# The start of an output projection: three hyena halves first, and the norm of y by token sums

## The chip, the core and the metric

The kernel runs on one core of one Trainium2 chip. The metric is the device time of one execution in microseconds (us). Engines: PE is TensorE (PEld its weight loads), DVE is VectorE, ACT is ScalarE, POOL is GpSimd, SP only issues DMAs.

## What is computed

Two layers of a block over 512 latent and 256 context tokens, width 1024. Layer 0 mixes by a bidirectional state-space scan (y) and by a long convolution (g, "hyena"), layer 1 by windowed attention; both end with a gated feed-forward. The change lies in `finish` of layer 0 and in how the first products after a norm are ordered:

```python
def finish(y, z, hy):
    b, L = z.shape[:2]
    y = rmsnorm(y.reshape(b, L, SSD_WIDTH) * jax.nn.silu(z.astype(jnp.float32)), norm_g).astype(z.dtype)
    g = hyena_op(hy, hy_conv_w, hy_conv_b, hy_filt, hy_bias)
    return jnp.concatenate([y, g], axis=-1) @ w_out
# rmsnorm(t, g) = t * rsqrt(mean(t*t, over the width) + 1e-6) * g
# x = x + mod * finish(...); then a norm with gains and shifts, then swiglu
```

## The kernel before

**Products in three parts.** Activations lie transposed: 8 tiles (`KT`) of 128 features by 768 tokens (`TOK`; `SEGS` cuts them into 512 and 256 columns). A float32 product is made of three: weights and activations are each split into a high part (rounded, fp32r) and a low part (the rest), and high x high, high x low and low x high are added in PSUM. `tiles` is that loop: for each tile four matmuls with the high part of the activations, then two with the low part. Eight tiles are called a half here.

**Weight jobs.** `JOBS` lists the weights in the order of use, 16 tiles a job in two halves, loaded by SP into one of 3 slots. VectorE makes the high half (`split_high`, `next_high`, the cast at L1587) in one buffer `WH` of two halves: a half can be cast only when the half of the job before has been multiplied (semaphore `blocks_done`). GpSimd makes the low half (`low`, L2013). TensorE waits for it in `half_ready` and for the PSUM accumulator in `pair_ready` (three accumulators, pairs 0 to 2). An "out0" job is one block of 128 output features: first half of the hyena input, second half of y. For other jobs (`two_blocks`) the halves are two blocks with the same input. `by_tile` gives a pair of waits per tile, for the high part (ScalarE) and the low part (GpSimd) of the input, used where the input is only being made.

**The order around the output projection.** Each engine's program is written out by hand; it runs in order.
- ScalarE copies the 8 high parts of g (L1362), squares the 8 tiles of y (L1368, two buffers), takes the root over 128x768 (L1370), then copies the high parts of the normed y (L1373).
- VectorE, after the scan, casts both halves for block 0, makes the 8 gate products y * silu(z) (L1813), waits for the root, takes the reciprocal (L1815) and multiplies each tile of y by gain and norm (L1817). Then `res` adds each block to the residual (L1844) and its squares to a running sum (L1510, L1511).
- GpSimd makes both low halves of weights for block 0, the 8 low parts of g and the 8 of y (L2155), then low halves one by one.
- TensorE multiplies block 0's hyena half, sums the squares over features with a matrix of ones (`norm_sums`, L551, 32 matmuls, the result on all partitions), multiplies block 0's half of y, then blocks 1 to 7.

**Other norms** use `norm_sum`: the squares summed in `T[:, 3]` are reduced per token by 6 small matmuls (L560) to 12 columns, root and reciprocal work on these, and 6 matmuls with the identity (L565) spread the result into PSUM (`NP`). VectorE then multiplies tile by tile (L1576) and applies gain and shift (L1578); ScalarE and GpSimd make the high (L1184) and low parts (L2026), and the first job behind it takes them with `by_tile`, its second block after its first.

Of the kernel before, what the change touches and what calls it, by code (L numbers as in the profile page):

```python
# [6 lines left out]
D = 1024  # L7
# [71 lines left out]
def plan():  # L79

    used, turn, out, last = [0, 0, 1], 0, [], None
    for kind, layer, _ in JOBS:
# [72 lines left out]
def build_kernel(nc, A, out):  # L155
# [6 lines left out]
    with ctx:  # L162
# [155 lines left out]
        def dvec(name, base, i, step=1):  # L318
# [16 lines left out]
            sq_ready sq_mm norm_sqrt norm_mul hn_ready conv_first  # L335
# [10 lines left out]
         sq_ready, sq_mm, n_sqrt, n_mul, hn_ready, cv_act,  # L346
# [115 lines left out]
        def _(pe):  # L462
# [31 lines left out]

            def two_blocks(gs, i, rhs, segs=SEGS, between=None, by_tile=None):
                for b in range(2):
                    half_ready(gs, i, b)
                    u = pair_ready(gs, i, b)
                    tiles(gs, pair(u), b, KT, rhs, segs, True, True, by_tile if b == 0 else None)
                    if b == 0 and between:  # L500
                        between()
# [44 lines left out]
            def norm_sums(segs=SEGS):  # L546

                for k in range(KT):
                    pe.wait_ge(sq_ready, k + 1)
                    for a, b in segs:  # L550
                        ins = mm(NP[:, a:b], C[:, ONES, :], T[:, k % 2, a:b], start=k == 0, stop=k == KT - 1)  # L551
                    ins.then_inc(sq_mm, 1)

            def norm_sum(n, segs=SEGS):
# [3 lines left out]
                pe.wait_ge(sums_ready, n + 1)  # L558
                for t in range(tiles):
                    ins = mm(NS[:, 2 * t:2 * t + 2], T[:, 3, t * P:t * P + P], C[:, ONES, 0:2],  # L560
                             start=True, stop=True)
                ins.then_inc(n_summed, 1)
                pe.wait_ge(n_rec, n + 1)
# [3 lines left out]
                ins.then_inc(n_spread, 1)  # L567
# [330 lines left out]
            def turn(s0, chunks, last):  # L898

                for d in range(2):  # L900
# [38 lines left out]
            half_ready([G0], 0, 0)  # L939
            first = pair(pair_ready([G0], 0, 0))  # L940
            tiles([G0], first, 0, KT, mixed, SEGS, True, False, mixed_waits)

            norm_sums()
            half_ready([G0], 0, 1)
            tiles([G0], first, 1, KT, lambda k: mixed(KT + k), SEGS, False, True,
                  [lambda k, wait=wait: wait(KT + k) for wait in mixed_waits])

            def res_block(name, rhs, segs=SEGS, by_tile=None, skip=0):
                def body(gs, i, r):
                    if isinstance(r, int) and r < skip:  # L950
                        return
# [3 lines left out]
            res_block("out0", mixed, by_tile=mixed_waits, skip=1)  # L955
# [140 lines left out]
        def _(act):  # L1096
# [266 lines left out]

            for k in range(KT):
                act.wait_ge(yz_ready, k + 1)
                if k >= 2:
                    act.wait_ge(sq_mm, k - 1)
# [106 lines left out]
        def _(dve):  # L1474
# [337 lines left out]
            for k in range(KT):  # L1812
                TT(XBC[:, k, :], XBC[:, k, :], Z[:, k, :], ALU.mult).then_inc(yz_ready, 1)  # L1813
            dve.wait_ge(n_sqrt, 2)
            ch.link(dve.reciprocal(T[:, 3, :], T[:, 2, :]))  # L1815
            for k in range(KT):
                STT(XBC[:, k, :], XBC[:, k, :], vec("sng", k), T[:, 3, :], ALU.mult, ALU.mult).then_inc(n_mul, 1)  # L1817
# [5 lines left out]
            def res(name, layer, m, segs, squares=True):  # L1823
# [5 lines left out]

                def body(gs, i, r):  # L1830
                    if not two:
                        next_high(gs, i, 0)
                    for b in range(2 if two else 1):
                        if two or b == 0:
                            next_high(gs, i, b if two else 1)
                        k = r if not two else 2 * r + b
# [6 lines left out]
                        for j, (a, e) in enumerate(segs):  # L1843
                            ins = STT(x[:, a:e], pair(u)[:, a:e], column(layer, m, k, j), x[:, a:e],  # L1844
                                      ALU.mult, ALU.add)
                        ins.then_inc(pair_free[u], 1)
# [6 lines left out]
                else:  # L1853
                    peel = 2 if name == "out0" else 0
                    job_turns(dve, name, 8, body, ch, 2 * SLOTS if squares else 0, peel)
# [114 lines left out]
        def _(pool):  # L1970
# [179 lines left out]

            for n in range(2 * KT):
# [4 lines left out]
            next_low("out0", 8, 2)  # L2156
# [98 lines left out]
def _layout(a):  # L2255
# [7 lines left out]
    for g, (kind, layer, n) in enumerate(JOBS):  # L2263
# [13 lines left out]
        elif kind == "out0":  # L2277
            wall[g] = np.roll(tiles(a["hy_out_w"][0], n * P), KT, 1)
            continue
        elif kind == "up":  # L2280
# [68 lines left out]
```

## Time and profile before

| | before |
|---|---|
| median of 3 runs | 2413.69 us |
| lowest, highest | 2411.80, 2418.44 us |
| profiled execution | 2418.78 us |
| its span (first to last instruction) | 2417.0 us |
| busy: PE, PEld, DVE, ACT, POOL | 92, 72, 40, 17, 35% |
| granted TensorE clock, mean of the span | 0.933 of 2.4 GHz |

Times in the rows count from the start of the span. A timeline row gives start, duration, engine, line, operation, output and inputs, count, and in brackets how long the engine idled before and what released it; a row with a count above 1 merges neighbours, and its duration is that of all. The end of a matmul is modelled, so neighbours overlap a little.

### The profile page before, as it was taken

How to read it: one execution, taken by the hardware profiler on the slowest of the kernel's cores; microseconds unless marked ns; L12 is line 12 of the kernel's file. 1: busy time of each engine (PE TensorE's matmuls, PEld its weight loads, DVE VectorE, ACT ScalarE, POOL GpSimd, SP SyncE). 2: the span in 40 equal slices, each digit the busy share in tenths (PEclk: the TensorE clock that was granted, in tenths of full speed). 3: DMA queues.
4: the chain of work that ended last, by engine and by line, in shares of the span. 5: the costliest groups of instructions: out<-in, count | busy, mean ns of one | idle time of the engine just before them, and what ended most of it. 6: DMA issues, size and time to landing. Idle time of an engine off the chain costs nothing. (4 is left out here: it accounts for less than half of the span.)

```text
span 2417.0 us, 30280 instructions
## 1 busy us (share of the span) xinstructions
PE 2217.1 (92%) x11978; PEld 1734.4 (72%) x11978; DVE 960.0 (40%) x1284; ACT 413.7 (17%) x769; POOL 856.9 (35%) x460
## 2 busy tenths in 40 slices
PE   7959998899998996997999999998787998999997
PEld 2436865688887774885888888887475666888886
DVE  3555354321234767335122112133525655322334
ACT  1211111001244553001000000000103631100110
POOL 0264353512223756323222332222421124444442
PEclk8777998999998997997999999999788998999998
DMA  8312432333311001110111221112110002223222
GB/s 302 135 52 96 152 111 101 107 113 126 102 44 53 1 2 43 56 67 26 61 61 48 74 71 61 53 60 70 61 45 18 1 28 69 95 78 112 91 82 73
DMA packets 50750, 181.52 MB, mean 75 GB/s; under 512 B 5815, under 2 KB 6071, under 8 KB 49688
## 3 DMA queue, kind: packets, MB, share of 16 engines
q1 hardware_dynamic: 48288, 163.60, 20.2%
q10 hardware_dynamic: 1848, 13.52, 1.5%
q0 software_dynamic: 512, 2.95, 0.3%
q8 instruction: 75, 1.23, 0.2%
q14 instruction: 27, 0.22, 0.0%
HBM read 177.95 MB, written 2.10 MB: 74 GB/s over the span
## 5 line engine op out<-in xcount | busy, mean ns | idle before, releaser
L2013 POOL TENSOR_TENSOR weights_lo<-weights,weights_hi 128x1024 fp32r<-128x1024 f32 (+1 forms) x232 | 514.4, 2218 | 1042.8 <-DVE weights_hi L1587 1042.8
L492 PE MATMUL psum<-normed_lo,weights_hi 128*128 128x512 f32 x1856 | 550.9, 360 | 12.0 <-POOL normed_lo L2026 11.9
L1587 DVE CAST weights_hi<-weights 128x1024 fp32r<-128x1024 f32 (+1 forms) x232 | 163.9, 707 | 921.1 <-PE psum L492 786.4
L487 PE MATMUL psum<-normed_hi,weights_hi 128*128 128x512 f32 (+1 forms) x1152 | 425.2, 369 | 16.1 <-ACT normed_hi L1184 16.1
L488 PE MATMUL psum<-normed_hi,weights_lo 128*128 128x512 f32 (+1 forms) x1152 | 404.8, 365 | 0.0
L492 PEld LDWEIGHTS psum<-normed_lo,weights_hi 128*128 128x128 f32 x1856 | 306.0, 193 | 43.7 <-POOL normed_lo L2026 26.3
L487 PEld LDWEIGHTS psum<-normed_hi,weights_hi 128*128 128x128 f32 x1152 | 221.6, 192 | 74.4 <-ACT normed_hi L1184 15.2
L487 PE MATMUL psum<-normed_first_hi,weights_hi 128*128 128x512 f32 x704 | 248.5, 353 | 16.1 <-POOL weights_lo L2013 9.3
L488 PEld LDWEIGHTS psum<-normed_hi,weights_lo 128*128 128x128 f32 x1152 | 222.7, 193 | 38.3 <-issue 1.5
L488 PE MATMUL psum<-normed_first_hi,weights_lo 128*128 128x512 f32 x704 | 226.7, 343 | 0.0
L487 PE MATMUL psum<-hidden_hi,weights_hi 128*128 128x512 f32 (+1 forms) x528 | 189.1, 358 | 0.0
L488 PE MATMUL psum<-hidden_hi,weights_lo 128*128 128x512 f32 (+1 forms) x528 | 178.9, 354 | 0.0
L487 PEld LDWEIGHTS psum<-normed_first_hi,weights_hi 128*128 128x128 f32 x704 | 135.8, 193 | 57.3 <-issue 10.8
L492 PE MATMUL psum<-hidden_lo,weights_hi 128*128 128x512 f32 (+1 forms) x528 | 160.4, 358 | 0.0
L488 PEld LDWEIGHTS psum<-normed_first_hi,weights_lo 128*128 128x128 f32 x704 | 136.3, 194 | 17.6 <-issue 1.2
L487 PEld LDWEIGHTS psum<-hidden_hi,weights_hi 128*128 128x128 f32 x528 | 99.1, 188 | 23.5
L488 PEld LDWEIGHTS psum<-hidden_hi,weights_lo 128*128 128x128 f32 x528 | 99.3, 188 | 15.0
L487 PE MATMUL psum<-mixed_hi,weights_hi 128*128 128x512 f32 (+1 forms) x256 | 90.5, 354 | 14.2 <-ACT mixed_hi L1373 8.0
L1618 DVE SCALAR_TENSOR_TENSOR temps<-psum,vectors,temps 128x511 f32<-128x511 f32 x112 | 63.8, 612 | 98.6 <-ACT temps L1198 97.6
L492 PEld LDWEIGHTS psum<-hidden_lo,weights_hi 128*128 128x128 f32 x528 | 87.1, 188 | 8.9
L1389 ACT ACTIVATE temps<-psum 128x768 f32<-128x768 f32 (+1 forms) x44 | 31.1, 707 | 355.7 <-PE psum L492 355.7
L1393 ACT ACTIVATE hidden_hi<-temps 128x768 f32 (+3 forms) x44 | 32.5, 740 | 342.9 <-DVE temps L1872 342.9
(281 smaller groups left out, 3015.1 us busy)
## 6 DMA issues: line engine op xcount, KB each, us to landing
weights<-in_wall SPq DMA_DIRECT2D x264, 512.0 KB, 4.0
weights<-in_wall SPq DMA_DIRECT2D x32, 384.0 KB, 3.2
weights<-in_wall SPq DMA_DIRECT2D x32, 320.0 KB, 3.0
residual<-in_xT ACTq DMA_DIRECT2D x2, 3072.0 KB, 10.4
phase<-in_tab ACTq DMA_DIRECT2D x3, 1280.0 KB, 7.0
out_T<-normed SPq DMA_DIRECT2D x2, 1024.0 KB, 4.3
normed<-in_window ACTq DMA_DIRECT2D x1, 1536.0 KB, 16.7
normed<-in_window POOLq DMA_DIRECT2D x1, 1536.0 KB, 7.7
```

What stands on the lines that cost most here:

```text
L487: mm(acc[:, lo:hi], WH[:, b, k, :], high[:, lo:hi], start=st, stop=False)
L488: mm(acc[:, lo:hi], WL[:, s, HALF * b + k, :], high[:, lo:hi], start=False, stop=False)
L492: ins = mm(acc[:, lo:hi], WH[:, b, k, :], low[:, lo:hi], start=False, stop=en)
L1389: run(T[:, 0, lo:hi], pair(0)[:, lo:hi], ACT.Silu).then_inc(pair_free[0], 1)
L1393: run(at_row(HIDH, r)[:, lo:hi], T[:, 1, lo:hi], ACT.Copy).then_inc(hid_hi, 1)
L1587: dve.tensor_copy(WH[:, b, 0:n, :], W[:, s, HALF * b:HALF * b + n, :]).then_inc(w_hi, 1)
L1618: ins = STT(t[:, a:e], p[:, a + shift:e + shift], w, t[:, a:e], ALU.mult, ALU.add)
L2013: TT(WL[:, s, at, :], W[:, s, at, :], WH[:, b, 0:width(gs[0], b), :].bitcast(f32), ALU.subtract).then_inc(w_lo, 1)
```

## The change

1. **Jobs.** The first three out0 jobs become "halves" jobs: (hyena of block 0, hyena of block 1), (hyena of block 2, y of block 0), (y of block 1, y of block 2). Blocks 3 to 7 follow as before, as stage out0b.
2. **Both blocks by tile.** `both_by_tile` takes two accumulators and does the first six tiles for both halves, then tiles 6 and 7 for the one and for the other. It serves the first halves job and, through `two_blocks(..., by_tile=...)`, the first job of the first stage, of the q projection and of each feed-forward's up projection.
3. **Norm of y by token sums.** ScalarE squares y into PSUM (`NP` and `TP` in turn), VectorE adds the squares into `T[:, 3]`, TensorE reduces them behind tile 5 and spreads the reciprocal root behind tile 7 of the first half. `norm_sums` and the work on 128x768 go. VectorE multiplies with the norm in PSUM.
4. **Order.** GpSimd waits for all gate products before its first low part of g. The low halves for the second job stand behind y's low parts 2 and 4 on GpSimd, and their casts behind y's tiles 2 and 4 on VectorE.

The number of products is the same. The diff, cut to its core:

```diff
-    stage("out0", [("out0", 0, n) for n in range(8)])
+    stage("out0", [("halves", 0, ((0, 1), (1, 1))), ("halves", 0, ((2, 1), (0, 0))), ("halves", 0, ((1, 0), (2, 0)))])
+    stage("out0b", [("out0", 0, n) for n in range(3, 8)])
...
+            def both_by_tile(gs, i, rhs, segs, by_tile, after=None, last=True, together=6):
+                s = gs[0] % SLOTS
+                accs = []
+                for b in range(2):
+                    half_ready(gs, i, b)
+                    accs.append(pair(pair_ready(gs, i, b)))
+                order = [(k, (0, 1)) for k in range(together)] + [(k, (b,)) for b in range(2) for k in range(together, KT)]
+                for k, blocks in order:
+                    if blocks[0] == 0:
+                        by_tile[0](k)
+                    high, low = rhs(k)
+                    for b in blocks:
+                        for lo, hi in segs:
+                            mm(accs[b][:, lo:hi], WH[:, b, k, :], high[:, lo:hi], start=k == 0, stop=False)
+                            mm(accs[b][:, lo:hi], WL[:, s, HALF * b + k, :], high[:, lo:hi], start=False, stop=False)
+                    if blocks[0] == 0:
+                        by_tile[1](k)
+                    for b in blocks:
+                        for lo, hi in segs:
+                            ins = mm(accs[b][:, lo:hi], WH[:, b, k, :], low[:, lo:hi], start=False,
+                                     stop=last and k == KT - 1)
...
-            norm_sums()
...
+            def between_tiles(k, blocks):
+                if k == 5 and blocks == (0, 1):
+                    pe.wait_ge(yz_sums, 1)
+                    token_sums(6).then_inc(yz_summed, 1)
+                if k == 7 and blocks == (0,):
+                    pe.wait_ge(yz_rec, 1)
+                    token_spread(6).then_inc(yz_spread, 1)
+            both_by_tile([G0], 0, mixed, SEGS, mixed_waits, between_tiles, False)
+            half_ready([G0 + 1], 0, 0)
+            pe.wait_ge(yz_added, KT)
+            tiles([G0 + 1], pair(pair_ready([G0 + 1], 0, 0)), 0, KT, mixed, SEGS, True, False)
+            for g, b, u in ((G0 + 1, 1, 0), (G0 + 2, 0, 1), (G0 + 2, 1, 2)):
+                half_ready([g], 0, b)
+                tiles([g], pair(u), b, KT, gated, SEGS, False, True, gated_waits if u == 0 else None)
...
-                run(T[:, k % 2, :], XBC[:, k, :], ACT.Square).then_inc(sq_ready, 1)
-            act.wait_ge(sq_mm, KT)
-            run(T[:, 2, :], NP, ACT.Sqrt, scale=1.0 / D, bias=vec("eps", 0)).then_inc(n_sqrt, 1)
+                run(TP if k % 2 else NP, XBC[:, k, :], ACT.Square).then_inc(yz_square, 1)
+            act.wait_ge(yz_summed, 1)
+            root()
```

On GpSimd, from the end of the scan, the program was this (`weights_lo`: low halves; `hyena_lo`, `ssd_lo`: low parts of g and of y):

```order
L2013 TENSOR_TENSOR weights_lo<-weights,weights_hi 128x1024 [waits weights_hi_ready] x2
L2155 TENSOR_TENSOR hyena_lo<-phase,mixed_hi 128x768 [waits mixed_hi] x8
L2155 TENSOR_TENSOR ssd_lo<-phase,mixed_hi 128x768 [waits mixed_hi] x8
L2013 TENSOR_TENSOR weights_lo<-weights,weights_hi 128x1024 [waits weights_hi_ready] x4
```

and is now, at the same place of the same engine:

```order
L2086 TENSOR_TENSOR weights_lo<-weights,weights_hi 128x1024 [waits weights_hi_ready] x2
L2229 TENSOR_TENSOR hyena_lo<-phase,mixed_hi 128x768 [waits mixed_hi,yz_ready]
L2229 TENSOR_TENSOR hyena_lo<-phase,mixed_hi 128x768 [waits mixed_hi] x7
L2229 TENSOR_TENSOR ssd_lo<-phase,mixed_hi 128x768 [waits mixed_hi] x3
L2086 TENSOR_TENSOR weights_lo<-weights,weights_hi 128x1024 [waits weights_hi_ready]
L2229 TENSOR_TENSOR ssd_lo<-phase,mixed_hi 128x768 [waits mixed_hi] x2
L2086 TENSOR_TENSOR weights_lo<-weights,weights_hi 128x1024 [waits weights_hi_ready]
L2229 TENSOR_TENSOR ssd_lo<-phase,mixed_hi 128x768 [waits mixed_hi] x3
```

The first low part of g has a wait for the gate products (`yz_ready`), and two low halves of weights have moved in between the low parts of y.

On VectorE, from the casts behind the scan (`phase` holds y, `temps` and `psum` the norm), the program was:

```order
L1587 CAST weights_hi<-weights 128x1024 [waits w_loaded11]
L1813 TENSOR_TENSOR phase<-phase 128x768 x8
L1815 RECIPROCAL temps<-temps 128x768 [waits norm_sqrt]
L1817 SCALAR_TENSOR_TENSOR phase<-phase,vectors,temps 128x768 [waits dve_order]
L1817 SCALAR_TENSOR_TENSOR phase<-phase,vectors,temps 128x768 x7
```

and is now:

```order
L1632 CAST weights_hi<-weights 128x1024 [waits w_loaded11]
L1858 TENSOR_TENSOR phase<-phase 128x768 x8
L1866 COPY temps<-psum 128x768 [waits yz_square]
L1864 TENSOR_TENSOR temps<-temps,psum 128x768 [waits yz_added,yz_square] x7
L1869 MEMSET mark 128x1 [waits yz_added]
L1871 RECIPROCAL temps<-temps 128x12 [waits norm_sqrt]
L1874 SCALAR_TENSOR_TENSOR phase<-phase,vectors,psum 128x768 [waits yz_spread]
L1874 SCALAR_TENSOR_TENSOR phase<-phase,vectors,psum 128x768 x2
L1632 CAST weights_hi<-weights 128x1024 [waits w_loaded20,blocks_done]
L1874 SCALAR_TENSOR_TENSOR phase<-phase,vectors,psum 128x768 x2
L1632 CAST weights_hi<-weights 128x1024 [waits w_loaded21,blocks_done]
L1874 SCALAR_TENSOR_TENSOR phase<-phase,vectors,psum 128x768 x3
```

Eight operations on the squares have come in, the reciprocal has shrunk to 12 columns, the norm is read from PSUM, and two casts stand between the multiplications.

## Rows read from the trace of the kernel before

**Rows 1.** Page, part 1: busy us, share of the span, instructions.
```profile
PE 2217.1 (92%) x11978; PEld 1734.4 (72%) x11978; DVE 960.0 (40%) x1284; ACT 413.7 (17%) x769; POOL 856.9 (35%) x460
```
**Rows 2.** Waits, 905 to 975: us in total, times, longest.
```profile
PE psum L492 <- POOL hyena_lo L2155: 9.0, 7, 3.9
```
**Rows 3.** Timeline of TensorE, 905 to 975: start us, us.
```profile
909.47 0.79 PE L487 MATMUL psum<-mixed_hi,weights_hi 128*128 128x512 f32 x1 [4.39 <-POOL weights_lo L2013]
...
932.64 10.86 PE L551 MATMUL psum<-temps,consts 128*128 128x512 f32 x32
951.50 0.77 PE L487 MATMUL psum<-mixed_hi,weights_hi 128*128 128x512 f32 x1 [8.00 <-ACT mixed_hi L1373]
...
972.98 0.47 PE L487 MATMUL psum<-mixed_hi,weights_hi 128*128 128x512 f32 x1 [1.78 <-POOL weights_lo L2013]
```
**Rows 4.** Busy time by stretch, then the cast behind the projection's last matmul.
```profile
core 0: us, PE busy (x) PEld busy (x) DVE busy (x) ACT busy (x) POOL busy (x), PEclk, DMA share, GB/s
...
1000.00:1092.00 92.00, 92.00 (x527) 80.41 (x527) 28.84 (x31) 0.00 (x0) 26.50 (x11) 1.00 0.19 63
...
1092.42 0.69 DVE L1587 CAST weights_hi<-weights 128x1024 fp32r<-128x1024 f32 x1 [7.62 <-PE psum L492]
```
**Rows 5.** VectorE: timeline, then L1817 by line (ns min/median/max, starts).
```profile
907.13 21.08 DVE L1813 TENSOR_TENSOR phase<-phase 128x768 f32<-128x768 f32 x8
944.47 4.95 DVE L1815 RECIPROCAL temps<-temps 128x768 f32<-128x768 f32 x1 [16.26 <-ACT temps L1370]
...
L1817 DVE SCALAR_TENSOR_TENSOR phase<-phase,vectors,temps x8: 1012/2572/2584, 949.5 to 962.3; 128x768 f32<-128x768 f32 x8
```
**Rows 6.** Timeline of VectorE and GpSimd, 970 to 997.
```profile
971.24 2.15 DVE L1587 CAST weights_hi<-weights 128x1024 fp32r<-128x1024 f32 x1 [4.18 <-PE psum L492]
...
992.23 1.14 DVE L1844 SCALAR_TENSOR_TENSOR residual<-psum,mods,residual 128x512 f32<-128x512 f32 x2
...
995.65 0.96 DVE L1511 TENSOR_TENSOR temps<-temps 128x768 f32<-128x768 f32 x1
...
992.39 2.40 POOL L2013 TENSOR_TENSOR weights_lo<-weights,weights_hi 128x1024 fp32r<-128x1024 f32 x1 [5.94 <-DVE weights_hi L1587]
```
**Rows 7.** GpSimd: timeline, then L2155 by line.
```profile
906.69 5.75 POOL L2013 TENSOR_TENSOR weights_lo<-weights,weights_hi 128x1024 fp32r<-128x1024 f32 x2 [3.11 <-DVE weights_hi L1587]
912.40 19.25 POOL L2155 TENSOR_TENSOR hyena_lo<-phase,mixed_hi 128x768 fp32r<-128x768 f32 x8
...
L2155 POOL TENSOR_TENSOR hyena_lo<-phase,mixed_hi x8: 1817/2528/2538, 912.4 to 929.8; 128x768 fp32r<-128x768 f32 x8
```
**Rows 8.** Timeline: a square of y; sums and spread of a later norm.
```profile
935.86 0.84 ACT L1368 ACTIVATE temps<-phase 128x768 f32<-128x768 f32 x1 [0.45 <-PE psum L551]
...
1097.69 2.72 PE L560 MATMUL psum<-consts,temps 128*128 128x2 f32 x12 [5.31 <-DVE mark L1858]
1101.04 2.93 PE L565 MATMUL psum<-consts,temps 128*128 128x128 f32 x12 [0.62 <-DVE temps L1568]
```
**Rows 9.** Busy time by stretch, after the idle 8 us.
```profile
950.00:960.00 10.00, 7.13 (x19) 5.40 (x20) 10.00 (x7) 4.35 (x6) 8.57 (x4) 0.50 0.00 0
```
**Rows 10.** Timelines: next job's first low half and first matmul, four norms.
```profile
212.92 2.40 POOL L2013 TENSOR_TENSOR weights_lo<-weights,weights_hi 128x1024 fp32r<-128x1024 f32 x1 [6.27 <-DVE weights_hi L1587]
...
218.87 0.50 PE L487 MATMUL psum<-normed_first_hi,weights_hi 128*128 128x512 f32 x1
...
1134.17 2.40 POOL L2013 TENSOR_TENSOR weights_lo<-weights,weights_hi 128x1024 fp32r<-128x1024 f32 x1 [1.88 <-DVE weights_hi L1587]
...
1142.32 0.39 PE L487 MATMUL psum<-normed_hi,weights_hi 128*128 128x512 f32 x1
...
1724.39 2.39 POOL L2013 TENSOR_TENSOR weights_lo<-weights,weights_hi 128x1024 fp32r<-128x1024 f32 x1 [3.62 <-DVE weights_hi L1587]
...
1728.19 0.40 PE L487 MATMUL psum<-normed_hi,weights_hi 128*128 128x512 f32 x1
...
2038.58 2.38 POOL L2013 TENSOR_TENSOR weights_lo<-weights,weights_hi 128x1024 fp32r<-128x1024 f32 x1 [1.36 <-DVE weights_hi L1587]
...
2043.18 0.39 PE L487 MATMUL psum<-normed_hi,weights_hi 128*128 128x512 f32 x1
```

More of the change, by code:

```diff
@@ L81, in plan @@
     used, turn, out, last = [0, 0, 1], 0, [], None
-    for kind, layer, _ in JOBS:
+    for kind, layer, what in JOBS:
+        if kind == "halves":
+            out.append([(block, used[block]) for block, hyena in what if hyena])
+            for block, hyena in what:
+                used[block] += hyena
+            last = kind
+            continue
         n = job_blocks(kind)
@@ L498, in two_blocks @@
                     u = pair_ready(gs, i, b)
-                    tiles(gs, pair(u), b, KT, rhs, segs, True, True, by_tile if b == 0 else None)
+                    tiles(gs, pair(u), b, KT, rhs, segs, True, True)
                     if b == 0 and between:
@@ L558, in norm_sum, with token_sums @@
                 pe.wait_ge(sums_ready, n + 1)
+                token_sums(tiles).then_inc(n_summed, 1)
+                pe.wait_ge(n_rec, n + 1)
+                token_spread(tiles).then_inc(n_spread, 1)
+            def token_sums(tiles):
                 for t in range(tiles):
@@ L561, in norm_sum, with token_spread @@
                              start=True, stop=True)
-                ins.then_inc(n_summed, 1)
-                pe.wait_ge(n_rec, n + 1)
+                return ins
+            def token_spread(tiles):
                 for t in range(tiles):
@@ L1813, in _ @@
                 TT(XBC[:, k, :], XBC[:, k, :], Z[:, k, :], ALU.mult).then_inc(yz_ready, 1)
+            for k in range(KT):
+                dve.wait_ge(yz_square, k + 1)
+                square = TP if k % 2 else NP
+                if k:
+                    dve.wait_ge(yz_added, k)
+                    ins = TT(T[:, 3, :], T[:, 3, :], square, ALU.add)
+                else:
+                    ins = dve.tensor_copy(T[:, 3, :], square)
+                ins.then_inc(yz_added, 1)
+            dve.wait_ge(yz_added, KT)
+            dve.memset(MARK[:, 0:1], 0.0).then_inc(yz_sums, 1)
             dve.wait_ge(n_sqrt, 2)
-            ch.link(dve.reciprocal(T[:, 3, :], T[:, 2, :]))
+            dve.reciprocal(RS[1][:, 0:12], RS[0][:, 0:12]).then_inc(yz_rec, 1)
+            dve.wait_ge(yz_spread, 1)
             for k in range(KT):
-                STT(XBC[:, k, :], XBC[:, k, :], vec("sng", k), T[:, 3, :], ALU.mult, ALU.mult).then_inc(n_mul, 1)
+                STT(XBC[:, k, :], XBC[:, k, :], vec("sng", k), NP, ALU.mult, ALU.mult).then_inc(n_mul, 1)
+                if k in (2, 4):
+                    next_high([G0], 0, k // 2 - 1)
             def column(layer, m, k, j):
@@ L1828, in res, with residual @@
                     ch.link(dve.memset(T[:, 3, lo:hi], 0.0))
+                def residual(x, u, k):
+                    for j, (a, e) in enumerate(segs):
+                        ins = STT(x[:, a:e], pair(u)[:, a:e], column(layer, m, k, j), x[:, a:e],
+                                  ALU.mult, ALU.add)
+                    ins.then_inc(pair_free[u], 1)
+                if name == "out0":
+                    next_high([G0 + 1], 0, 0)
+                    next_high([G0 + 1], 0, 1)
+                    for k in range(3):
+                        residual(X[:, k, :], k, k)
+                        read([G0 if k < 2 else G0 + 1], 0, k if k < 2 else 0, dve)
+                        ch.link(add_squares(X[:, k, :], lo, hi))
+                        if k < 2:
+                            next_high([G0 + 2], 0, k)
                 def body(gs, i, r):
@@ L1835, in body @@
                             next_high(gs, i, b if two else 1)
-                        k = r if not two else 2 * r + b
+                        k = r + 3 if name == "out0" else r if not two else 2 * r + b
                         if two:
@@ L1842, in body @@
                             dve.wait_ge(blocks_done, 2 * len(JOBS))
[L1843 to L1846, printed above, removed]
+                        residual(x, u, k)
                         if squares:
@@ L2155, in _ @@
                 TT(YGL[j][:, k, :], src, YGH[:, j, k, :].bitcast(f32), ALU.subtract).then_inc(mix_lo, 1)
-            next_low("out0", 8, 2)
+                if n in (KT + 2, KT + 4):
+                    low([G0 + 1], 0, (n // 2 - 5,))
+            for g in (G0 + 1, G0 + 2):
+                low([g + 1], 0)
+            next_low("out0b", 5)
             def out_low(item):
@@ L2279, in _layout @@
             continue
+        elif kind == "halves":
+            two = [(a["hy_out_w"][0][D * hyena:D * hyena + D], block * P) for block, hyena in n]
         elif kind == "up":
```

41 lines of the change are left out of this document (19 added, 22 removed).

## The prediction, made before the changed kernel was run

> **What bounds the kernel now.** I read the busy shares first: TensorE is busy for 92% of the span [rows 1], so what can be won is the time in which it waits, or runs at its lower clock. Then the waits of TensorE in the stretch where the output projection of layer 0 begins: the largest is for the low parts of the hyena output, 9.0 us in 7 waits [rows 2]. Then the timeline of that stretch, engine by engine.
>
> TensorE starts block 0 at 909.5, needs until 932.6 for its first half, sums the squares of y for 10.9 us, idles 8.0 us, starts the second half at 951.5 and block 1 at 973.0 [rows 3]. A half is 8 tiles of 6 matmuls. With TensorE busy throughout at a granted clock of 1.00 (2.4 GHz) it takes 8.4 us: the stretch 1000 to 1092 is 92.00 of 92.00 us busy with 527 matmuls, 48 to a half [rows 4]; it ends with the projection. So two halves, 16.8 us of work, have taken 63.5 us.
>
> Why: VectorE's eight gate products take 21.1 us [rows 5], 2.6 each, while GpSimd works; the same form alone, two inputs in SBUF, takes 0.96 [rows 6]. GpSimd's low parts take 2.5 us beside them and 1.82 alone [rows 7]. Then the norm: a reciprocal of 128x768, 4.95 us, and eight multiplications, 2.57 us as a rule and 1.01 the shortest, again against GpSimd [rows 5, 7]. But an operation of VectorE with one input in PSUM is not slowed: the residual STT at 992.23 takes 1.14 us for both segments inside a low part of 2.40 us [rows 6].
>
> **The change, part by part.** All times are on the clock of the profiled execution.
>
> Start. TensorE now needs both low halves of the weights before its first matmul; the second is done at 912.4 [rows 7], so it starts 3.0 us later than at 909.5.
>
> Gate products. GpSimd still splits the weights until 912.4, beside the first two products, which end at 912.8 as before. It then waits for all eight. Six products at 0.96 end at 918.6. Queued behind GpSimd's wait are all its low parts, and TensorE waits for the first: it comes at 918.6 + 1.82 = 920.4, where it came at 914.9 (TensorE's wait on it is in [rows 2]). The eight low parts end at 918.6 + 8 x 1.82 = 933.2, against 931.6. So this edit alone costs TensorE's first tile 5.5 us; its price is paid by the norm, which comes earlier.
>
> Norm. ScalarE squares into PSUM in 0.84 [rows 8], VectorE adds eight times with one input in PSUM. That form (TT, one input in PSUM) is nearest to the residual STT, not slowed; I take 0.96 to 1.0 each, so the sums are ready at 918.6 + 8 x 0.97 = 926.4. The upper bound is 2.6 each, 939.4, as for two inputs in SBUF [rows 5]. The 32 matmuls of 10.9 us fall away. For them come two groups of six small ones (each in two passes, so 12 records): the same groups at a later norm take 2.7 and 2.9 us [rows 8], with matmuls that go at 1.2 GHz there; at 2.4 I take half, 2.9 together. The square root and the reciprocal are now 12 columns; they lie beside tiles 6 and 7 (2.1 us), and the 4.95 us reciprocal goes.
>
> TensorE's 16 tile halves. A tile half is 1.05 us at 2.4 GHz [rows 4], at 1.2 twice that. The high part of tile 0 for both blocks is done before 920.4 (1.3 tile halves), so 14.7 are left. After an idle time the clock is low: 950 to 960, after the 8.0 us, was granted 0.50 though TensorE was busy for 7.13 us of it [rows 9]. I take 6 us at 1.2 GHz (2.9 tile halves) and 11.8 x 1.05 = 12.4 us at 2.4, with 2.9 for the small matmuls: the end is 920.4 + 6 + 12.4 + 2.9 = 941.7. GpSimd at 1.82 per tile is ahead of TensorE at 2.1. The spread, on which VectorE's multiplications wait, is done two tile halves before the end, at 939.6. Call it S.
>
> The new wait. TensorE's next half (block 2, hyena) needs a low half of weights, which GpSimd makes behind three low parts of y. VectorE: three STTs with the norm in PSUM at 1.0 (the fastest of the eight was that long) to S + 3.0, then the cast. A cast that met GpSimd took 2.15 against 0.69 alone [rows 4, 6], so S + 4.5 to 5.2; not critical. ScalarE's first copy ends at S + 2.0. GpSimd: three low parts to S + 7.5, of which one loses 0.6 to 0.7 to the cast, then 2.4 for the weights, again with up to 0.7 for the second cast: S + 10.5 to 11.2. I take 10.9. TensorE resumes at 950.5 after 8.8 us idle. Here the Trainium skill speaks against the two casts: SBUF — State Buffer, Who interferes with whom, says that VectorE and GpSimd share one pair of ports as an exclusive lock, and that the one which comes second is fully blocked. By that rule neither cast could slip in beside a low part and the forecast would be 2383; the trace's two casts agree with it (2.15 against 0.69 us).
>
> After it 14 halves, 117.6 us. Nothing of them waits: every cast is released by the end of a half, and cast and low part (3.1 us) lie beside the next half of 8.4. The second half of that job (y for block 0) needs y's last low part at about S + 23, and starts at S + 10.9 + 8.4 = S + 19 with its first tiles. The restart at 1.2 GHz costs 2.5 us (5 us at half speed). End: 950.5 + 117.6 + 2.5 = 1070.6. Before, the 14 halves went from 973.0 to 1092.4, 119.4 us; the cast that waits for the last matmul is the last of [rows 4]. **Gain 21.8 us.** DMAs: SP's queue has the same loads in the same order; the weights of the second and third of the new jobs are loaded at the end of the scan as now, and the next load waits for the first of the 16 tile halves' blocks, some 20 us before its cast. GpSimd's queue is moved past no DMA.
>
> The four starts after a norm. Now the first job of the first stage, of the two feed-forwards and of the q projection does both blocks on each of the first six tiles. The tiles still come as VectorE and GpSimd give them (both unchanged), so block 0 ends when it did, and block 1 ends two tile halves later instead of eight. But the next job needs its low half of weights, which hangs on block 0's end alone and stays where it is. The gain is thus the next job's start less the end of that low half [rows 10]:
> - first stage: 218.87 - 215.32 = 3.5, less some 1.5 for a clock that falls in the 4 us of waiting: 2.0. This low half hangs on a load that is issued at block 0's end.
> - feed-forward 0: 1142.32 - 1136.57 = 5.7; the wait is short, the clock stays.
> - q projection: 1728.19 - 1726.78 = 1.4, less 1.4 for the clock: 0. VectorE is held up there by a wait for the rope table before its cast, not by TensorE.
> - feed-forward 1: 2043.18 - 2040.96 = 2.2.
>
> Sum 9.9 us; its ends are 3 (clock falls at each) and 13 (nowhere).
>
> Total 21.8 + 9.9 = 31.7 us. The span of 2417.0 becomes 2385.3, the execution of 2418.8 becomes 2387.1. That execution is 5.1 above the median of the runs (2413.7), so the forecast for the median is 2382.0.
>
> **The rivals.**
> *VectorE and GpSimd still collide* with PSUM inputs, or the wait for the gate products does not do what it says. For it: every SBUF pair is slowed. Against: the STT at 992.23 [rows 6]. Then the adds last to 939.4, TensorE waits for the sums before tile 6, S comes near 945.5 and the restart at S + 13, 958.5: 8 us less, 2390. The gate wait useless (products slow anyway, 2.6 each) would give the same order, 9.6 us.
> *The starts give nothing*, since the low half of the next weights comes later or the clock falls in each: 2392. Against: block 0's last tile is paced as before.
> *The clock stays up* through the wait for weights and in every start: 5 us more, 2376. The row of 950 to 960 speaks against it.
> *Slower*: the restart after 8.8 us of idle doesn't bring the clock back. Place: the 14 halves behind 950.5. A half at 1.2 GHz costs 8.4 us more; from the fourth such half on (31.7 / 8.4 = 3.8) the kernel is slower than before, and with all 14 it is 2497. Against: after the 8.0 us idle in the trace, and with a TensorE that was still waiting for tiles, the clock was 1.00 again from 1000 on [rows 4, 9].
>
> **How the numbers follow.** Main case 0.66 (2374 to 2390). Collision 0.13 (2390), starts give nothing 0.10 (2392), clock stays up 0.07 (2376), slower 0.02, small effect through something unseen 0.02. The predicted time is the main case's 2382. The range 2372 to 2396 takes in all but the last two and the tails of the first ones. A measurement here can tell about 0.3%, 7 us: faster than 2406.5 in 0.95, within 0.3% in 0.03, slower in 0.02.
>
> **What would show it.** Gate products of about 2.6 us for two and 0.96 for six; adds and STTs of about 1 us beside low parts of 1.82; the sums in TensorE behind tile 5 without a wait; an idle time of 8 to 9 us before block 2, released by the low weights; last matmul of the projection some 22 us earlier; second jobs behind the norms released by the low weights. It would be wrong if the adds take over 2 us, or if TensorE's clock in the 16 tile halves stays at 1.2 GHz (12 us more), or if the starts show the same times for the second jobs.

## The result, and the profile after

The changed kernel takes **2384.24 us** (median of 4 runs, 2383.03 to 2385.71) against 2414.68 for the kernel before, run beside it (2411.80 to 2418.44). The ratio is 0.9865, its 95% interval 0.9849 to 0.9880: 30.4 us less, against a forecast of 2382.0 in a range of 2372 to 2396. A second set of four runs, e12 below, gave 2383.82.

The profiled execution took 2385.36 us, its span 2383.5 against 2417.0 before. The first two lines are part 1 of its page (as [rows 1]) and the row of TensorE's granted clock in 40 slices; then come TensorE's four longest waits between 895 and 1064 us (engine, line, releaser: us in total, times, longest), as [rows 2]:

```profile
PE 2180.6 (91%) x11970; PEld 1720.1 (72%) x11970; DVE 950.4 (40%) x1293; ACT 413.2 (17%) x770; POOL 848.9 (36%) x460
...
PEclk7879999899998997998999999998898998999998
...
PE psum L495 <- POOL weights_lo L2086: 8.5, 1, 8.5
PE psum L518 <- POOL weights_lo L2086: 7.6, 1, 7.6
PE psum L524 <- POOL hyena_lo L2229: 4.9, 1, 4.9
PE psum L924 <- DVE normed L1805: 1.2, 1, 1.2
```

TensorE is busy for 36.5 us less; its idle time has hardly moved (199.9 us before, 202.9 after). The seven waits for low parts of g are one, and the long wait is now for the weights of block 2, as forecast.

TensorE's timeline of the stretch (start us, us), the counterpart of [rows 3]. L518, L519 and L524 are tiles of the first job, L596 the token sums, L602 the spread, L495 the first tile of block 2, L1632 (VectorE) the cast that opens the stage:

```profile
906.84 0.76 PE L518 MATMUL psum<-mixed_hi,weights_hi 128*128 128x512 f32 x1 [7.56 <-POOL weights_lo L2086]
...
914.60 1.65 PE L524 MATMUL psum<-hyena_lo,weights_hi 128*128 128x512 f32 x4 [4.86 <-POOL hyena_lo L2229]
...
928.64 1.39 PE L596 MATMUL psum<-consts,temps 128*128 128x2 f32 x12
...
932.08 1.50 PE L602 MATMUL psum<-consts,temps 128*128 128x128 f32 x12
...
944.22 0.79 PE L495 MATMUL psum<-mixed_hi,weights_hi 128*128 128x512 f32 x1 [8.52 <-POOL weights_lo L2086]
```

VectorE and GpSimd beside it, the counterparts of [rows 5, 7]:

```profile
900.11 1.29 DVE L1632 CAST weights_hi<-weights 128x1024 fp32r<-128x1024 f32 x2
901.32 11.33 DVE L1858 TENSOR_TENSOR phase<-phase 128x768 f32<-128x768 f32 x8
912.57 0.95 DVE L1866 COPY temps<-psum 128x768 f32<-128x768 f32 x1
913.63 7.31 DVE L1864 TENSOR_TENSOR temps<-temps,psum 128x768 f32<-128x768 f32 x7
921.00 0.06 DVE L1869 MEMSET mark<- 128x1 f32 x1
930.37 0.23 DVE L1871 RECIPROCAL temps<-temps 128x12 f32<-128x12 f32 x1 [9.31 <-ACT temps L1222]
933.62 2.87 DVE L1874 SCALAR_TENSOR_TENSOR phase<-phase,vectors,psum 128x768 f32<-128x768 f32 x3 [3.02 <-PE psum L602]
936.40 1.56 DVE L1632 CAST weights_hi<-weights 128x1024 fp32r<-128x1024 f32 x1
...
939.73 2.22 DVE L1632 CAST weights_hi<-weights 128x1024 fp32r<-128x1024 f32 x1
...
912.73 14.40 POOL L2229 TENSOR_TENSOR hyena_lo<-phase,mixed_hi 128x768 fp32r<-128x768 f32 x8 [6.11 <-DVE phase L1858]
935.59 5.80 POOL L2229 TENSOR_TENSOR ssd_lo<-phase,mixed_hi 128x768 fp32r<-128x768 f32 x3 [8.46 <-ACT mixed_hi L1418]
941.37 2.80 POOL L2086 TENSOR_TENSOR weights_lo<-weights,weights_hi 128x1024 fp32r<-128x1024 f32 x1
```

The stage opens at 900.11 where it opened at 905.92, so 5.8 us must be taken off the prediction's times when they are laid beside these. The eight gate products take 11.33 us (21.08 before), the adds 7.31 / 7 = 1.04 us each beside low parts of 14.40 / 8 = 1.80. The sums are ready at 921.00, but TensorE comes to them at 928.64 only: 7.6 us to spare.

**Where the time went.** I cut the span at events that both kernels have: the token sums of the norms and the cast that opens the output projection. Three of these rows are

```profile
170.49 2.69 PE L596 MATMUL psum<-consts,temps 128*128 128x2 f32 x12 [10.90 <-POOL vectors L2078]
...
1068.86 2.72 PE L596 MATMUL psum<-consts,temps 128*128 128x2 f32 x12 [5.14 <-DVE mark L1931]
...
1986.19 1.87 PE L596 MATMUL psum<-consts,temps 128*128 128x2 f32 x8 [4.66 <-DVE mark L1931]
```

and the table has the differences. The last columns are the experiments' profiled executions ("6 tiles together": e2 to e5, e7 and e12; "4 together": e6 and e8 to e10); in them a stage whose code is the same shows how far one execution differs from another.

| stretch, us | before | after | e1: starts undone | e11: starts alone | others, first job of 6 tiles together | others, 4 together |
|---|---|---|---|---|---|---|
| up to the first token sums | 172.0 | 170.5 | 171.8 | 169.3 | 167.4 to 171.5 | 168.5 to 171.3 |
| first norm to the cast | 733.9 | 729.6 | 733.7 | 732.8 | 728.6 to 732.9 | 727.8 to 732.1 |
| cast to feed-forward 0 | 191.8 | 168.8 | 168.8 | 191.7 | 169.2, 169.9, unless edited | 168.9, unless edited |
| feed-forward 0 to q projection | 587.5 | 581.2 | 587.5 | 581.7 | 581.0 to 582.1 | 582.8 to 583.9 |
| q projection to feed-forward 1 | 334.1 | 336.1 | 333.5 | 336.6 | 332.0 to 337.8 | 330.5 to 333.7 |
| feed-forward 1 to the last sums | 383.8 | 383.5 | 383.9 | 383.5 | 382.4 to 384.3 | 381.9 |

Before less after: 1.6 + 4.3 + 23.0 + 6.3 - 2.0 + 0.4, with nothing behind the last sums, is the 33.5 us between the two spans, but for rounding. The 1.6 lie ahead of any changed instruction.

### The profile page after: what moved, and what is told of

Read it like the earlier page. It is cut to its first block and busy times, and to the rows that moved or that the text cites. A ratio compares the mean times of both kernels' runs of the same rounds, so it can differ in the third digit from the quotient of the medians.

```text
span 2383.5 us, 30200 instructions
## 1 busy us (share of the span) xinstructions
PE 2180.6 (91%) x11970; PEld 1720.1 (72%) x11970; DVE 950.4 (40%) x1293; ACT 413.2 (17%) x770; POOL 848.9 (36%) x460
## 5 line engine op out<-in xcount | busy, mean ns | idle before, releaser
L1632 DVE CAST weights_hi<-weights 128x1024 fp32r<-128x1024 f32 (+1 forms) x232 | 167.4, 723 | 900.8 <-PE psum L500 748.3
L500 PE MATMUL psum<-normed_lo,weights_hi 128*128 128x512 f32 x1760 | 508.5, 352 | 0.0
L495 PE MATMUL psum<-normed_hi,weights_hi 128*128 128x512 f32 x1088 | 395.4, 363 | 5.7 <-POOL weights_lo L2086 5.7
L496 PE MATMUL psum<-normed_hi,weights_lo 128*128 128x512 f32 x1088 | 373.9, 358 | 0.0
L500 PEld LDWEIGHTS psum<-normed_lo,weights_hi 128*128 128x128 f32 x1760 | 284.9, 190 | 16.8
L495 PEld LDWEIGHTS psum<-normed_hi,weights_hi 128*128 128x128 f32 x1088 | 206.4, 190 | 56.7 <-POOL weights_lo L2086 4.8
L495 PE MATMUL psum<-normed_first_hi,weights_hi 128*128 128x512 f32 (+1 forms) x672 | 234.0, 348 | 10.4 <-POOL weights_lo L2086 9.9
L496 PEld LDWEIGHTS psum<-normed_hi,weights_lo 128*128 128x128 f32 x1088 | 206.9, 190 | 35.5 <-issue 1.8
L496 PE MATMUL psum<-normed_first_hi,weights_lo 128*128 128x512 f32 (+1 forms) x672 | 214.6, 341 | 0.0
L495 PE MATMUL psum<-hidden_hi,weights_hi 128*128 128x512 f32 (+1 forms) x528 | 189.0, 358 | 0.0
L495 PEld LDWEIGHTS psum<-normed_first_hi,weights_hi 128*128 128x128 f32 x672 | 128.3, 191 | 46.2 <-POOL weights_lo L2086 12.0
L496 PEld LDWEIGHTS psum<-normed_first_hi,weights_lo 128*128 128x128 f32 x672 | 128.6, 191 | 16.4 <-issue 1.0
L495 PEld LDWEIGHTS psum<-hidden_hi,weights_hi 128*128 128x128 f32 x528 | 99.1, 188 | 23.4
L495 PE MATMUL psum<-mixed_hi,weights_hi 128*128 128x512 f32 x224 | 76.4, 341 | 8.5 <-POOL weights_lo L2086 8.5
```

The source lines that it names most:

```text
L495: mm(acc[:, lo:hi], WH[:, b, k, :], high[:, lo:hi], start=st, stop=False)
L496: mm(acc[:, lo:hi], WL[:, s, HALF * b + k, :], high[:, lo:hi], start=False, stop=False)
L500: ins = mm(acc[:, lo:hi], WH[:, b, k, :], low[:, lo:hi], start=False, stop=en)
L1632: dve.tensor_copy(WH[:, b, 0:n, :], W[:, s, HALF * b:HALF * b + n, :]).then_inc(w_hi, 1)
```

## The experiments

Each set of runs had its own runs of the kernel before, with medians of 2417.0 to 2417.2. The median of one kernel moves by up to 3 us between sets (before: 2414.7 in the first, 2417.2 in a later one), so below I give the stage's length in the profiled execution too, which is steadier: 168.8 to 169.9 us in the five executions whose output projection is that of the changed kernel.

**e1, the four starts undone.** `two_blocks` again does block 0 whole, then block 1:

```diff
-                if by_tile:
-                    both_by_tile(gs, i, rhs, segs, by_tile)
-                    return
+                    tiles(gs, pair(u), b, KT, rhs, segs, True, True, by_tile if b == 0 else None)
```

> The changed kernel, except that the four first jobs after a norm (first stage, both feed-forwards, q projection) do block 0 whole and then block 1, as before; the start of the output projection stays changed. My theory (the starts are worth what lies between the next job's low half and its first matmul): their share was 10 to 12 us (3.5 first stage, 5.6 and 2 to 3 the feed-forwards, about 0 the q projection), so this kernel takes 2394 to 2397 us against 2384 of the changed one. Rival (the starts give little and the output projection gave all 30 us): 2384 to 2387. In the trace the next jobs' first matmuls follow the low halves by 3.5, 5.7, 1.4 and 2.2 us again.

2394.11 us (2393.28 to 2394.86), ratio to before 0.9904 (0.9889 to 0.9919). That is 9.9 us over the changed kernel, where the prediction had 9.9 for the starts; the projection's stage is the same to 0.1 us. It rules out the rival, by which the output projection gave all 30 us.

**e11, the starts alone**, in the kernel before.

> The kernel before, with only the four first jobs after a norm done for both blocks on each of the first six tiles; the output projection is as before. If the two parts of the change are independent, this kernel is faster than the one before by what undoing them cost, 9.9 us: 2404 to 2408 us against 2414 to 2417. Rival (the starts win more when the projection is not changed, or nothing at all without it): outside 2402 to 2410.

2407.46 against 2417.15, ratio 0.9966 (0.9954 to 0.9978): 9.7 us, with an interval of 5 to 11. As far as that interval can tell, the two parts add up and do not lean on each other.

**e2, GpSimd does not wait for the gate products** (its `pool.wait_ge(yz_ready, KT)` is taken out).

> The changed kernel without GpSimd's wait for all eight gate products: it goes from the weights straight to the low parts. My theory (two inputs in SBUF collide with GpSimd, and the norm hangs on the products): the products take 21 us again instead of 11.3, the sums are ready some 9 us later, the first low part comes some 5.5 us earlier but this wins nothing, since TensorE waits before its seventh tile; about 2391 to 2393 us. Rival (products and low parts only swap places, TensorE gets its first tile 5.5 us earlier and keeps it): 2379 to 2384.

2392.29 us (2391.40 to 2395.85), ratio 0.9901 (0.9886 to 0.9917), 8 us more than with the wait. Its VectorE timeline, and TensorE's at the sums:

```profile
901.50 21.20 DVE L1858 TENSOR_TENSOR phase<-phase 128x768 f32<-128x768 f32 x8
...
931.16 2.72 PE L596 MATMUL psum<-consts,temps 128*128 128x2 f32 x12 [8.25 <-DVE mark L1869]
```

TensorE hardly waits for low parts of g (0.3 us in two waits, 4.9 in one with the gate wait) and gives it all back in a wait of 8.25 us at the sums. The stage is 174.8 us for 168.8, 6 of the 8 us. So the gate wait is a real part of the gain.

**e3, the squares in SBUF:**

```diff
-                run(TP if k % 2 else NP, XBC[:, k, :], ACT.Square)
+                run(T[:, k % 2, :], XBC[:, k, :], ACT.Square)
...
-                square = TP if k % 2 else NP
+                square = T[:, k % 2, :]
```

> The changed kernel with the squares of y written by ScalarE to two buffers in SBUF instead of PSUM, so that VectorE's adds have both inputs in SBUF. Nothing else differs. Collision theory: the adds go from 0.9 to 1.0 us to some 2.5 each and GpSimd's low parts of the hyena output beside them from 1.80 to some 2.5; the sums are ready some 11 us later (932 for 921 on the trace's clock), TensorE idles before its seventh tile, and the kernel takes 2393 to 2397 us. Rival (the place of the input does not matter, the adds were fast for another reason): 2384 to 2386, adds at 1.0 us.

2387.67 us (2386.39 to 2392.25), ratio 0.9877 (0.9862 to 0.9892): the mechanism is there, but the cost is 3.4 us by medians, where I had expected 9 to 13. The profiled execution is the slowest of the four, 2392.25 us.

```profile
913.21 17.45 DVE L1864 TENSOR_TENSOR temps<-temps 128x768 f32<-128x768 f32 x7
...
912.72 19.61 POOL L2229 TENSOR_TENSOR hyena_lo<-phase,mixed_hi 128x768 fp32r<-128x768 f32 x8 [6.11 <-DVE phase L1858]
...
930.84 2.72 PE L596 MATMUL psum<-consts,temps 128*128 128x2 f32 x12 [1.89 <-DVE mark L1869]
```

The adds take 2.49 us each instead of 1.0, the low parts beside them 2.45 instead of 1.80. Only the place of the squares differs, so this settles the collision. The Trainium skill (SBUF — State Buffer, Who interferes with whom) says that a VectorE instruction with two SBUF inputs contends with a GpSimd instruction that reads SBUF and that one with at most one SBUF input, outside the two-port modes, does not; both halves agree with this pair of runs. The sums are ready 9.7 us later (930.7 for 921.0), but 7.6 of them were to spare: TensorE starts them 2.2 us later. The rest of the stage's 6.5 us (175.2 for 168.8) is mostly its clock, low again for the sums (2.72 for 1.39 us) and the tiles behind them: the granted clock from 930 to 935 is 0.59, and 1.00 in the changed kernel. Why this execution lost 3 us more than the medians show is open. My expectation had charged the whole delay to TensorE.

**e4, the norm read from a copy in SBUF.** ScalarE copies `NP` to `T[:, 2, :]`, and VectorE's eight STTs read that.

> The changed kernel, but ScalarE first copies the spread norm from PSUM to SBUF, and VectorE's eight multiplications read the copy: both their tensors are then in SBUF. Collision theory: the three multiplications before GpSimd's first low part of y stay near 1 us, those beside low parts go to 2 to 2.6 us, and low parts of y beside them to some 2.5; with 1.0 us for the copy the restart of TensorE at block 2 comes 2 to 4 us later, which is 2386 to 2389 us. Rival (no collision): only the copy shows, 2385, multiplications at 1.0 us.

2388.66 us (2384.69 to 2390.85), ratio 0.9891 (0.9873 to 0.9909); the stage 172.0 us, 3.3 more.

```profile
932.25 2.88 DVE L1876 SCALAR_TENSOR_TENSOR phase<-phase,vectors,temps 128x768 f32<-128x768 f32 x3 [3.87 <-ACT temps L1417]
...
942.82 8.12 DVE L1876 SCALAR_TENSOR_TENSOR phase<-phase,vectors,temps 128x768 f32<-128x768 f32 x3
...
934.22 8.13 POOL L2231 TENSOR_TENSOR ssd_lo<-phase,mixed_hi 128x768 fp32r<-128x768 f32 x3 [9.30 <-ACT mixed_hi L1420]
...
945.15 0.80 PE L495 MATMUL psum<-mixed_hi,weights_hi 128*128 128x512 f32 x1 [11.68 <-POOL weights_lo L2088]
```

The three STTs that start before GpSimd does take 0.96 us each and the last three, beside it, 2.7 (0.95 with the norm in PSUM). GpSimd's three low parts take 8.13 instead of 5.80 us, and TensorE waits 11.68 instead of 8.52. Here nothing was to spare: of the 3.2 us, the copy is 0.8 (VectorE starts 34.4 us behind the stage's opening, 33.5 without it) and GpSimd's slower low parts are 2.3. By medians the cost is 4.4 us.

**e5, the weights of block 2 first:**

```diff
+            next_high([G0], 0, 0)
             dve.wait_ge(yz_spread, 1)
...
-                if k in (2, 4):
-                    next_high([G0], 0, k // 2 - 1)
+                if k == 2:
+                    next_high([G0], 0, 1)
...
-                if n in (KT + 2, KT + 4):
-                    low([G0 + 1], 0, (n // 2 - 5,))
+                if n in (KT - 1, KT + 1):
+                    low([G0 + 1], 0, (0 if n < KT else 1,))
```

> The changed kernel with the weights of block 2 split first: VectorE's cast comes before its first multiplication with the norm (not behind the third) and GpSimd's low half of them before the low parts of y (not behind the third); the second half of that job is cast behind the third multiplication and split behind the second low part of y. My theory (the 8.5 us in which TensorE idles before block 2 are GpSimd's chain of three low parts and the weights, counted from the spread of the norm): the idle time shrinks to 0 to 2 us, the clock does not fall, and TensorE loses up to 1 us to the low parts of y in the next half; 2373 to 2377 us. Rival (the time is only moved: y's last low parts come later and TensorE waits for them in the half of y of block 0): 2382 to 2385.

2377.37 us (2374.76 to 2380.18), ratio 0.9837 (0.9824 to 0.9851): 7 us faster than the changed kernel by medians (the two intervals just touch), and its stage is 161.8 us, 7.0 less.

```profile
933.15 0.69 DVE L1632 CAST weights_hi<-weights 128x1024 fp32r<-128x1024 f32 x1 [1.68 <-PE psum L524]
...
933.92 2.39 POOL L2087 TENSOR_TENSOR weights_lo<-weights,weights_hi 128x1024 fp32r<-128x1024 f32 x1 [5.92 <-DVE weights_hi L1632]
...
952.49 0.62 PE L500 MATMUL psum<-ssd_lo,weights_hi 128*128 128x512 f32 x2 [0.45 <-POOL ssd_lo L2230]
...
954.27 0.61 PE L500 MATMUL psum<-ssd_lo,weights_hi 128*128 128x512 f32 x2 [0.47 <-POOL ssd_lo L2230]
...
956.59 0.50 PE L495 MATMUL psum<-mixed_hi,weights_hi 128*128 128x512 f32 x1 [1.70 <-POOL weights_lo L2087]
...
930.00:940.00 10.00, 10.00 (x65) 8.94 (x65) 6.43 (x8) 2.99 (x5) 5.93 (x3) 1.00 0.32 104
```

The cast needs only block 0's end, not the norm. The 8.5 us idle are gone, TensorE is busy through 930 to 940 at a granted clock of 1.00, and 2.6 us come back in three waits of the next half, all of them for GpSimd, which is now the bound there.

**e6, four tiles together at the starts instead of six.**

> The changed kernel, but at the four starts behind a norm only the first four tiles, not six, are done for both blocks; block 1 then has four tile halves left behind block 0's end instead of two. My theory (the next job hangs on block 0's end, cast and low half, not on block 1): the next jobs start when they did, TensorE's waits before them (1.6, 0, 3.8 and 1.9 us) shrink to 0, 0, 1.7 and 0, and at most a clock that falls less gives 1 to 2 us: 2382 to 2385. Rival (what is left of block 1 is on the path): 2.1 us more at each start, 2388 to 2392.

2383.06 us (2379.88 to 2389.64), ratio 0.9867 (0.9844 to 0.9890): no difference in total, but some that cancel. Feed-forward 1 gains 1.8 us on average (381.9, in all four kernels with this edit): its wait of 1.88 became 0.56 and the clock stayed at 1.00. The q projection's stretch is 330.8 us, against 332.9 to 337.8 with six. Feed-forward 0 loses 1.7 (583.2 for 581.5 on average): there TensorE does block 1's four last tile halves from 1107.9 to 1113.9, the first two of them at 1.2 GHz, 1.92 us each, while the low half of the next weights is done at 1111.3. So they outlast it by 2.6 us. That is the rival's mechanism, at one of the four starts.

**e7, the rope table early**: its load ahead of the low parts, VectorE's wait for it behind the first q job's casts.

> The changed kernel with the rope table loaded before the low parts of the q projection's norm instead of behind them, and VectorE's wait for it behind the casts of the first q job instead of ahead of them. My theory (the q start gave nothing, since the wait for the table held the cast for some 2.5 us): the cast follows the end of block 0 directly, the next q job's low half ends 2 to 2.5 us earlier, TensorE waits 1 to 1.5 us in place of 3.8, and the kernel takes 2380 to 2382 us. Rival (the casts wait for something else): 2384.

2380.60 us (2378.82 to 2390.24), ratio 0.9862 (0.9841 to 0.9884). By medians that is 3 to 4 us less than the changed kernel; by the ratio the two can't be told apart. TensorE's wait before the second q job:

```profile
1690.53 0.79 PE L495 MATMUL psum<-normed_hi,weights_hi 128*128 128x512 f32 x1 [0.68 <-POOL weights_lo L2087]
```

It is 0.68 for 3.84 us, so the table did hold the cast.

**e8, e5 to e7 together.**

> The changed kernel with three edits together: weights of block 2 cast and split ahead of y, only four tiles for both blocks at the starts, and the rope table early with VectorE's wait for it behind the casts. If their effects add up, the time is that of the changed kernel less 7 us for the first, less 0 to 2 for the second and 2 to 4 for the third: 2371 to 2375 us. Rival (what one wins is lost again at the other places): 2376 to 2378.

**2372.43 us** (2369.71 to 2374.86), ratio 0.9823 (0.9808 to 0.9837), 12 us below the changed kernel and within the 2371 to 2375 of effects that add up. Neither e9 nor e10 can be told from it.

**e9 and e10** edit e8 further: GpSimd waits for six gate products instead of eight; VectorE makes the last two low parts of y.

> The kernel with the three edits together, in which GpSimd waits for six gate products, not eight. The squares' sums were ready some 6 us before TensorE came to them. My theory (that spare time can be spent): the first low part comes 1.9 us earlier, two gate products beside low parts take 2.5 us instead of 0.96, the sums are ready 3 us later, still before TensorE's seventh tile, and the stage is shorter by 1.5 to 1.9 us: 2370 to 2371.5 us. Rival (TensorE at its lower clock is what paces the tiles, so an earlier first tile is given back in waits): 2372 to 2373.5.

> The kernel with the three edits together, in which VectorE, not GpSimd, makes the last two of y's eight low parts, behind its cast for block 1. After the cast is moved ahead, TensorE waits 0.45, 0.47 and 1.70 us for GpSimd's low parts and weights in the next half. My theory (GpSimd is the bound there, busy from 934 to 957 without a gap): its queue gets 3.6 us shorter, VectorE's two take 1 to 2.5 us each in its idle time, the three waits shrink to under 1 us together: 1.5 to 2.5 us less, 2370 to 2371. Rival (VectorE's operations hold up GpSimd's by as much as they take off it): 2372 to 2373.5.

e9 2372.78 us (0.9816, 0.9798 to 0.9833), e10 2372.31 us (0.9817, 0.9797 to 0.9837). Both medians lie in the range that I had given to the rivals. In its own trace each shortens the stage, from 161.0 to 159.6 and 159.8 us, which is less than I wanted and about as much as one and the same stage moves from one execution to another: neither theory nor rival is shown. In e10 VectorE's two low parts take 5.10 us, 2.55 each beside GpSimd; TensorE's waits in that half shrink from 2.6 to 0.8 us, as expected, but the stage gets only 1.2 shorter.

**e12, the changed kernel again.**

> The changed kernel once more, unchanged, beside the others, to see how far its median moves from one set of runs to the next. If such a median is good to 1.5 us: 2382.5 to 2386. Rival (sets of runs differ by more, and differences of 3 us between kernels of different sets mean nothing): outside that.

2383.82 us (2381.99 to 2384.84), within what was expected of a second set. The kernel before moved by more: 2414.68 in the first set, 2417.15 in this one.

## Why the prediction held, point by point

**The total.** The gain is 30.4 us by the first set and 33.3 by the last (2417.15 less 2383.82), for a forecast of 31.7. The forecast of the time itself took off 5.1 us, by which the profiled execution of the kernel before lay above the median of three runs. Above the later medians of 9 and 17 runs, 2417.0 to 2417.2, it lies by only 1.7, and with these the same gain would have given 2385.4. So which of the two comes nearer to the measured 2384.2 says nothing of the mechanism; the parts do.

**The projection: 23.0 us for a forecast of 21.8.** Laid beside the prediction's times less 5.8, nearly every step is where it was put: first low part used at 914.60 (914.6), sums ready at 921.00 (920.6), spread read from 933.62 (S = 933.8), restart 944.22 (944.7) after 8.52 us idle (8.8). The two casts slipped in at 1.56 and 2.22 us, and GpSimd lost 0.4 us to each, so the restart lies 10.6 us behind the spread for 10.9 forecast. Steps that stood on one row of another operation held: the adds were not slowed, as the residual STT was not, and e3 shows that it is the place of the squares; the STTs took 1.0, and e4 shows the same of the norm. That the chain of three low parts and the weights is behind the 8.5 us is shown by e5, which took it away.

**The gate wait** paid for itself as argued (e2), through the sums and not through the low parts.

**The collision rival** was priced at 8 us on the assumption that both adds and STTs collide. e3 and e4 together cost 6.5 + 3.3 us of stage and 3.4 + 4.4 by medians, so its size was about right. Alone, the adds cost less than their delay, since 7.6 us were to spare. The rival in the prediction already had this: its sums are 13 us later, but its spread only 5.9 (945.5 for 939.6; e3 has 5.5). It is my expectation for e3 that forgot it and charged TensorE with the whole delay.

**The starts: the sum is right, two of its terms are not.** e1 and e11 give 9.9 and 9.7 us for a forecast of 9.9. By stage, on average, they were 3.2 in the first (733.8 in the two executions with the old order, 730.6 the mean of twelve with a new one; forecast 2.0), 6.0 in feed-forward 0 (587.5 for 581.5; forecast 5.7), -1.6 in the q projection (333.8 in two, 335.4 the mean of seven), within its scatter (0), and 0.1 in feed-forward 1 (2.2). These add up to 7.7, which the interval of e11 (5 to 11) takes in; that the medians met 9.9 to a tenth is luck. The failed step is who pays for the clock. Lines of the changed kernel at the first stage and at feed-forward 1 (in the stretches, the second number behind the times is TensorE busy, and third from the end is the granted clock):

```profile
213.83 0.50 PE L495 MATMUL psum<-normed_first_hi,weights_hi 128*128 128x512 f32 x1 [1.62 <-POOL weights_lo L2086]
...
214.00:219.00 5.00, 5.00 (x29) 4.39 (x30) 2.04 (x1) 0.00 (x0) 3.98 (x2) 1.00 0.91 287
...
2008.06 0.49 PE L495 MATMUL psum<-normed_hi,weights_hi 128*128 128x512 f32 x1 [1.88 <-POOL weights_lo L2086]
...
2007.00:2012.00 5.00, 3.94 (x12) 3.13 (x13) 3.79 (x3) 0.63 (x1) 3.31 (x2) 0.74 0.48 165
2012.00:2017.00 5.00, 5.00 (x22) 4.01 (x21) 0.69 (x1) 0.60 (x1) 0.62 (x1) 0.92 0.05 9
```

- I charged the first stage 1.5 us, for a clock that falls in 4 us of waiting. In nine of the twelve executions TensorE waits 2.0 us or less there and the clock stays at 1.00; in the other three (e2, e5, e11) it waits 3.1 to 3.4 us, and the 5 us behind the wait are at 0.68. The cast that lies 179.0 us behind the token sums with the old order lies at 175.5 to 176.0 in the nine and at 176.9 to 177.2 in the three. So the forecast's 3.5 and 2.0 are both there, and it had picked the rarer one.
- I charged feed-forward 1 nothing. It starts its next job 2.0 us earlier and loses that again: in seven of the eight executions with six tiles together the clock falls behind the wait of 1.9 us. In the eighth (e3) it stays at 1.00 behind the same wait, and that stretch is the shortest of the eight, 382.4 us for 383.5 to 384.3 (383.8 and 383.9 with the old order). e6 shows it from the other side.

The two errors have opposite signs: the first stage gave 1.2 us more than forecast, feed-forward 1 gave 2.1 less. The old order has only two such executions, so the split between the first stage and the q projection is good to some 2 us, no better.

**The slower rival** did not come: after 8.52 us idle the first 3.8 us were at 1.2 GHz (forecast: 5), and then the clock was back. This row is of the first 10 us behind 950; the two after it are at 1.00 as well.

```profile
950.00:960.00 10.00, 10.00 (x58) 8.72 (x57) 1.45 (x1) 0.00 (x0) 7.92 (x5) 1.00 0.17 54
```

## What to carry to other kernels

Before a new wait or a slower operation is priced, find the moment at which the consumer asks: in e3 a delay up to that moment was free, and what exceeded it cost its length and a spell at the lower clock. When TensorE idles behind a queue, ask what the item it needs really depends on; here the next weights needed the end of a block and stood behind three operations that needed the norm, and putting them first was worth 7 us. Beside a working GpSimd, give VectorE's operations on two tensors one input in PSUM; here that was worth 3.4 to 6.5 us for the adds and 2.4 to 3.6 for the multiplications, depending on whether one goes by the medians or by the stage, and with the copy taken off.

## What the hardware showed beyond expectation

The two engines all but take turns: in e3 VectorE's SBUF add takes 2.49 us and GpSimd's low part beside it 2.45, where 0.96 and 1.81 alone, one after the other, would be 2.77. So a pair of streams that collide runs at nearly the speed of one engine doing both.

In feed-forward 1 a wait of 1.9 us was enough, in seven of eight executions, for TensorE to fall to 1.2 GHz, though it had been busy but for 0.3 us from 1992.9 to 2006.2 in the changed kernel; the clock fell when it had been at work again for over 1 us. In the first stage waits of up to 2.0 us were not enough, and those of 3.1 us and more were. Why the one and not the other stays open.
